# Two latent up-projections on whole float32 operands in place of split halves

## The reference

```
def rmsnorm(x, g):
    x32 = x.astype(jnp.float32)
    y = x32 * lax.rsqrt(jnp.mean(x32 * x32, axis=-1, keepdims=True) + EPS)
    return y.astype(x.dtype) * g
...
        h = rmsnorm(x, pre_norm_mix[l])
        proj = h @ w_in[l]
        g_a, g_b, qa, ka, va, cq, ckv, kr = jnp.split(proj, SPLIT_IDX, axis=-1)
...
        out_a = swa_sink_alibi_attention(qa, ka, va, positions, sinks[l])
        qb = (rmsnorm(cq, q_a_norm[l]) @ w_q_b[l]).reshape(B, S, N_HEADS_B, Q_HEAD_B)
        kvb = (rmsnorm(ckv, kv_a_norm[l]) @ w_kv_b[l]).reshape(B, S, N_HEADS_B, KV_HEAD_B)
        q_nope, q_rope = qb[..., :QK_NOPE], rope(qb[..., QK_NOPE:], positions)
        k_nope, v_b = kvb[..., :QK_NOPE], kvb[..., QK_NOPE:]
        k_rope = rope(kr[:, :, None, :], positions)[:, :, 0, :]
        out_b = mla_attention(q_nope, q_rope, k_nope, k_rope, v_b)
```

## Time and profile before

| what | value |
|---|---|
| median of three runs | 1555.5 us (1555.41 to 1556.49) |
| the profiled execution's own time | 1553.86 us |
| its span | 1552.1 us |
| mean granted TensorE clock | 0.946 |
| busy: PE, DVE, POOL, ACT | 1351.1, 998.1, 628.8, 546.2 us |
| DMA | 397.56 MB, mean 256 GB/s |

### The profile page before, as it was taken

One profiled execution on the slowest core, in us unless ns is written; L12 is line 12 of the kernel. 1 busy time (PEld: TensorE's weight loads), 2 busy tenths in 40 slices (PEclk: granted clock), 3 DMA queues, 4 the chain that ended last, 5 costly groups with the idle time before them and its releaser, 6 DMA issues. The chain is left out here.

```text
span 1552.1 us, 26715 instructions
## 1 busy us (share of the span) xinstructions
PE 1351.1 (87%) x10416; PEld 1296.6 (84%) x10416; DVE 998.1 (64%) x2056; ACT 546.2 (35%) x984; POOL 628.8 (41%) x361
## 2 busy tenths in 40 slices
PE   7989998899898878696888787888898898799996
PEld 6989998898897878696878787888886678689996
DVE  4698946755478585858585859555647565584563
ACT  6444454444432121211112121211564464344341
POOL 1387742221365545454545454542147312122220
PEclk9999999899999989898989898999999999899998
DMA  7445452442359999999999999999342224145450
GB/s 289 148 163 189 172 200 95 163 163 102 114 232 420 422 421 422 422 422 421 422 421 421 420 421 422 422 421 421 139 138 82 82 104 141 50 156 202 164 190 27
DMA packets 58073, 397.56 MB, mean 256 GB/s; under 512 B 6272, under 2 KB 9856, under 8 KB 10368
## 3 DMA queue, kind: packets, MB, share of 16 engines
q0 software_dynamic: 36864, 268.45, 41.6%
q1 hardware_dynamic: 21120, 127.89, 23.2%
HBM read 395.27 MB, written 1.05 MB: 255 GB/s over the span
## 5 line engine op out<-in xcount | busy, mean ns | idle before, releaser
L449 POOL TENSOR_TENSOR w_lo<-raw,w_hi 128x2048 fp32r<-128x2048 f32 x62 | 287.2, 4634 | 570.8 <-ACT w_hi L903 524.2
L761 PE MATMUL bank<-h_norm,rows_late 128*128 128x128 f32 x2816 | 332.8, 281 | 27.1 <-ACT h_norm L1052 27.1
L761 PEld LDWEIGHTS bank<-h_norm,rows_late 128*128 128x128 f32 x2816 | 328.6, 198 | 30.5 <-ACT h_norm L1052 30.5
L1591 DVE SCALAR_TENSOR_TENSOR rows_late<-rows_late,squares 128x1024 f32<-128x1024 f32 x176 | 212.8, 1223 | 131.0 <-DMA rows_late<-peer_uv_dram,stage 129.3
L588 PE MATMUL bank<-x_hi_a,w_hi 128*128 128x256 f32 (+1 forms) x904 | 266.5, 295 | 20.0 <-DVE x_lo_a L1214 11.0
L589 PE MATMUL bank<-x_lo_a,w_hi 128*128 128x256 f32 (+1 forms) x904 | 258.9, 286 | 0.0
L590 PE MATMUL bank<-x_hi_a,w_lo 128*128 128x256 f32 (+1 forms) x904 | 258.9, 286 | 0.0
L761 PE MATMUL bank<-h_norm,rows_early 128*128 128x128 f32 x1280 | 179.5, 309 | 91.0 <-ACT h_norm L1052 90.9
L761 PEld LDWEIGHTS bank<-h_norm,rows_early 128*128 128x128 f32 x1280 | 173.2, 222 | 97.6 <-ACT h_norm L1052 97.6
L530 POOL DMA_INDIRECT rows_late<-peer_uv_dram,stage x165 | 195.1, 1183 | 132.7 <-PE bank L761 95.1
L903 ACT ACTIVATE w_hi<-raw 128x2048 fp32r<-128x2048 f32 (+1 forms) x119 | 224.3, 1887 | 52.7 <-PE bank L590 45.7
(11 more groups left out here) (278 smaller groups left out, 1902.4 us busy)
## 6 DMA issues: line engine op xcount, KB each, us to landing
raw<-w_in_dram SPq DMA_DIRECT2D x40, 1024.0 KB, 4.8
raw<-w_up_dram SPq DMA_DIRECT2D x16, 1024.0 KB, 4.8
raw<-w_down_dram SPq DMA_DIRECT2D x16, 1024.0 KB, 4.8
raw<-w_kv_dram SPq DMA_DIRECT2D x8, 1024.0 KB, 4.7
raw<-w_peer_q_dram SPq DMA_DIRECT2D x8, 1024.0 KB, 4.7
raw<-sc_w_out_dram SPq DMA_DIRECT2D x4, 1024.0 KB, 4.7
raw<-cf_w_pw_dram SPq DMA_DIRECT2D x4, 1024.0 KB, 4.7
raw<-w_mix_out_dram SPq DMA_DIRECT2D x4, 1024.0 KB, 4.8
```

What stands on the lines that cost most here:

```text
L449: api.tensor_tensor(ring(w_lo, i), ring(raw, i), ring(w_hi, i).bitcast(F32), ALU.subtract).then_inc(w_lo_ready[LO_BY[i][0]], 1)
L761: mm = nc.tensor.matmul(ct(Y_ACC[c][t // 4], t % 4, P), expert_rows(k)[:, D + t * P:D + (t + 1) * P], ct(diag, k % DIAGS, P), start=False, ...
L1591: w_.scalar_tensor_tensor(out=row, in0=row, scalar=1.0, in1=h_tok[:, c * D:(c + 1) * D], op0=ALU.mult, op1=ALU.mult, accum_out=pre[:, side ...
```

## The change

Loads 69 and 70 form the set WHOLE. They are still loaded into `raw` at their place in the order, but have no high and no low half. `kn`, `vb` and `qb` are computed by one float32 matmul per k-tile, from `raw` and from the normalised `c_kv` and `c_q`, in place of three float32r matmuls. TensorE now waits for the DMA and for the norm. ACT's two roundings of these loads and its roundings of the latents are gone, and so are DVE's two subtractions of the loads and its subtractions of the latents (`norm` in place of `norm_split`). The condition under which `raw` is filled again changes for the two loads that follow them in their slots, 72 and 73: the DMA waits for the last output tile that reads load 69 (`vb` 3) or load 70 (`qb` 7), in place of the low half. The counts of the semaphores follow (HI_COUNT, LO_BY).

```
--- before.py
+++ after.py
@@ -151,9 +151,14 @@
             + [("w_in_2", b) for b in (2, 3, 4, 5, 6, 7, 11)])
 BY_DVE = range(LOAD_OF["pq", 12], BEFORE_GATHERS + 3)
 
-LO_BY = []
+WHOLE = {i for i, (w, _) in enumerate(LOADS) if w in ("w_kv_b_2", "w_q_b_2")}
+LO_BY, HI_COUNT = [], []
 _seen = {"dve": 0, "pool": 0}
 for _i in range(len(LOADS)):
+    HI_COUNT.append(_i + 1 - sum(w <= _i for w in WHOLE))
+    if _i in WHOLE:
+        LO_BY.append(None)
+        continue
     _e = "pool" if _i % 3 == 2 and _i not in BY_DVE or LOADS[_i] in DVE_BUSY else "dve"
     _seen[_e] += 1
     LO_BY.append((_e, _seen[_e]))
@@ -176,8 +181,7 @@
 
 SPLITS = {"h1": (8, 0, 0, None), "mem": (8, 1, 0, None), "sc": (8, 0, 0, ("gcf", 7)), "pw": (8, 1, 0, ("k", 7)),
           "merge": (8, 0, 0, ("sc", 7)), "xa": (8, 1, 0, ("pw", 7)), "o": (8, 0, 0, ("mix", 7)),
-          "peer": (8, 1, 0, ("q", 7)), "h2": (8, 0, 0, ("xo", 7)), "kv": (1, 1, 0, ("pq", 15)),
-          "q": (2, 1, 1, ("pq", 15)), "oa": (4, 1, 0, ("qb", 7)), "ob": (4, 1, 4, ("qb", 7)),
+          "peer": (8, 1, 0, ("q", 7)), "h2": (8, 0, 0, ("xo", 7)), "oa": (4, 1, 0, ("qb", 7)), "ob": (4, 1, 4, ("qb", 7)),
           "wo": (8, 0, 0, ("gb", 7)), "mlp": (8, 1, 0, ("ob", 7)), "hid0": (FH, 2, 0, None),
           "hid1": (FH, 2, 0, ("down", 7))}
 SPLIT_ENDS = {}
@@ -443,7 +447,7 @@
 
         def w_lo_split(eng, api, i):
 
-            eng.wait_ge(w_hi_ready, i + 1)
+            eng.wait_ge(w_hi_ready, HI_COUNT[i])
             if i >= RING:
                 eng.wait_ge(acc_ready, LAST_TILE[i - RING] + 1)
             api.tensor_tensor(ring(w_lo, i), ring(raw, i), ring(w_hi, i).bitcast(F32),
@@ -461,8 +465,11 @@
                 name, b = LOADS[i]
                 if i >= RING:
 
-                    engine, n = LO_BY[i - RING]
-                    sp.wait_ge(w_lo_ready[engine], n)
+                    if i - RING in WHOLE:
+                        sp.wait_ge(acc_ready, LAST_TILE[i - RING] + 1)
+                    else:
+                        engine, n = LO_BY[i - RING]
+                        sp.wait_ge(w_lo_ready[engine], n)
                 sp.dma_start(ring(raw, i), T[name][b]).then_inc(raw_landed[i % RING], 16)
 
             sp.dma_start(vec[:], T["vecs"]).then_inc(vec_landed, 16)
@@ -504,7 +511,7 @@
 
             def subtract_to(last):
                 while n_lo[0] <= min(last, len(LOADS) - 1):
-                    if LO_BY[n_lo[0]][0] == "pool":
+                    if n_lo[0] not in WHOLE and LO_BY[n_lo[0]][0] == "pool":
                         w_lo_split(pool, g, n_lo[0])
                     n_lo[0] += 1
 
@@ -575,6 +582,12 @@
                 engine, n = LO_BY[i]
                 pe.wait_ge(w_lo_ready[engine], n)
                 return ring(w_hi, i), ring(w_lo, i)
+
+            def whole_slot(name, b):
+
+                i = LOAD_AT[name, b]
+                pe.wait_ge(raw_landed[i % RING], 16 * (i // RING + 1))
+                return ring(raw, i)
 
             def halves(x, k, cols=slice(0, SEQ)):
 
@@ -807,26 +820,28 @@
             linear("qa", range(2), "w_in_2", 8, "h2", DT, 256)
             stat_sq("q_a", mean_q)
             linear("qa", range(2, 4), "w_in_2", 9, "h2", DT, 256)
-            w = slot("w_kv_b_2", 0)
+            w = whole_slot("w_kv_b_2", 0)
+            pe.wait_ge(normed, NORMED["kv_a"])
             for h in range(HB):
                 out = open_tile("kn", h)
-                three(out[0:NOPE, 0:SEQ], [half[:, h * KVHB:h * KVHB + NOPE] for half in w], halves("kv", 0),
-                      True, True).then_inc(acc_ready, 1)
+                nc.tensor.matmul(out[0:NOPE, 0:SEQ], w[:, h * KVHB:h * KVHB + NOPE], c_kv[:],
+                                 start=True, stop=True).then_inc(acc_ready, 1)
             for c in range(NC):
                 for part in range(2):
                     out = open_tile("vb", 2 * c + part)
-                    three(out[:, :], halves("kv", 0, slice(c * P, (c + 1) * P)),
-                          [half[:, part * 512:(part + 1) * 512] for half in w], True, True).then_inc(acc_ready, 1)
+                    nc.tensor.matmul(out[:, :], c_kv[:, c * P:(c + 1) * P], w[:, part * 512:(part + 1) * 512],
+                                     start=True, stop=True).then_inc(acc_ready, 1)
             rot = k_of("rot")[NOPE:QHB, 0:QHB]
             wait_drained(pe, "kr", 0)
             out = open_tile("krot", 0)
             nc.tensor.matmul(out[0:QHB, 0:SEQ], rot, k_r[NOPE:QHB, :], start=True, stop=True).then_inc(acc_ready, 1)
-            w = slot("w_q_b_2", 0)
+            w = whole_slot("w_q_b_2", 0)
+            pe.wait_ge(normed, NORMED["q_a"])
             for h in range(HB):
                 out = open_tile("qb", h)
                 for k in range(2):
                     at = k * HB * QHB + h * QHB
-                    mm = three(out[0:QHB, 0:SEQ], [half[:, at:at + QHB] for half in w], halves("q", k), k == 0, k == 1)
+                    mm = nc.tensor.matmul(out[0:QHB, 0:SEQ], w[:, at:at + QHB], ct(c_q, k), start=(k == 0), stop=(k == 1))
                 mm.then_inc(acc_ready, 1)
 
             def beside_attention(i):
@@ -897,11 +912,13 @@
             def round_to(last):
                 while n_hi[0] <= min(last, len(LOADS) - 1):
                     i = n_hi[0]
+                    n_hi[0] += 1
+                    if i in WHOLE:
+                        continue
                     act.wait_ge(raw_landed[i % RING], 16 * (i // RING + 1))
                     if i >= RING:
                         act.wait_ge(acc_ready, LAST_TILE[i - RING] + 1)
                     s.activation(ring(w_hi, i), ring(raw, i), ACT.Copy).then_inc(w_hi_ready, 1)
-                    n_hi[0] += 1
 
             def normed_tile(norm_name):
                 first = NORMED[norm_name] - dict(NORMS)[norm_name]
@@ -1116,11 +1133,9 @@
                 drain("cq", i, ct(c_q, i))
             root("kv_a")
             square("q_a", drained_tile("cq"), c_q)
-            split_all("kv", normed_tile("kv_a"), c_kv)
             for i in range(2):
                 drain("qa", i, ct(q_a, i))
             root("q_a")
-            split_all("q", normed_tile("q_a"), c_q)
             for i in range(2, 4):
                 drain("qa", i, ct(q_a, i))
             for h in range(HB):
@@ -1242,7 +1257,7 @@
 
             def subtract_to(last):
                 while n_lo[0] <= min(last, len(LOADS) - 1):
-                    if LO_BY[n_lo[0]][0] == "dve":
+                    if n_lo[0] not in WHOLE and LO_BY[n_lo[0]][0] == "dve":
                         w_lo_split(dve, w_, n_lo[0])
                     n_lo[0] += 1
 
@@ -1683,9 +1698,9 @@
             ahead("ka", 0)
             ahead("ckv", 0)
             ahead("cq", 0)
-            norm_split("kv_a", c_kv, "kv_a_norm_2", c_kv, "kv")
+            norm("kv_a", c_kv, "kv_a_norm_2", c_kv)
             ahead("qa", 0)
-            norm_split("q_a", c_q, "q_a_norm_2", c_q, "q")
+            norm("q_a", c_q, "q_a_norm_2", c_q)
             ahead("qa", 2)
             ahead("kn", 0)
 
```

## The result

The changed kernel takes 1564.39 us (median of six runs, 1561.31 to 1570.94), the kernel before on the same chips 1556.28 us (six runs, 1555.41 to 1560.46). The ratio is 1.0054, with a 95% interval from 1.0037 to 1.0072. So it is slower by about 8 us, where 7.0 were forecast. A second set of six runs of the same file gave 1566.28 us and 1.0053 [1.0037, 1.0068].

What follows compares the result with a forecast made beforehand. TensorE's own work was taken to set the end of the stage. 5.3 us of stall, including 2.1 for float32 matmuls, plus 1.7 for the clock gave +7.0: 1562.5 us on the median, 8-in-10 range 1557.8 to 1566.

Steps and rivals of the forecast that it cites:

- The float32 pairs: In `kn`, `vb` and `qb`, two float32 matmuls replace three float32r ones: 0.43 against 0.36 us for narrow tiles, +2.1 us showing.
- the pause of 1.16 us: TensorE's wait ahead of `kn` 4 for ACT, which rounds load 71 first; it hides 0.3 us of the first four tiles.
- The four passes: Alternative price for the float32 matmuls in `kn`, `vb` and `qb`: four passes instead of three, 3.7 us in all; not adopted.
- The chain of steps 1 to 6: Last `vb` matmul, DMA of load 72, ACT's rounding, drain of `qb` 0, then `qb` 4: +5.3 us, matmuls' 2.1 included.
- the landing: Load 72's DMA, issued at 1149.4 behind `vb` 3, lands 4.8 us later at the median, at most 5.0.
- the clock: TensorE's 3.1 us pause in `qb` lowers its granted clock behind it: +1.7 us, bounds 0 and 3.4.
- the attention: Behind the changed stage, attention, output layers and MLP only shift along, since nothing downstream is tied to an absolute time.
- The rival of the clock that keeps its level: The wait in `qb` comes but the clock stays up in `qb` 4 to 7: +5.3 us, 1560.8 us; chance 0.2.
- the rival "faster": Attention gives time back and load 72's transfer costs less than its 4.8 us: 1553 to 1555 us; chance 0.04.
- The second late transfer: Loads 73, 74 and 75 issue together around `qb` 7; load 73 lands late, losing 1 to 4 us more; chance 0.14.
- The delay given back: In the attention, POOL's subtraction shifts against head a 1's scores, TensorE's 3.42 us gap shrinks: +1.9 us, 1557.4; chance 0.12.

Runs made afterwards that it cites:

- own buffers: Changed kernel with the two whole weights loaded into idle buffers of their own, so `raw` is refilled early again: 1559.93 us, ratio 1.0019 to the kernel before.
- The late refill without float32: Kernel before, keeping all its halves, with only loads 72 and 73 made to wait for the last tile of loads 69 and 70: 1562.75 us, ratio 1.0042.
- The drain put first: Changed kernel, load 72 still late, but ACT rounds it behind the drains of `qb`: 1563.1 us, ratio 1.003 to the kernel before.
- `w_kv_b_2` alone: Changed kernel with only `w_kv_b_2` multiplied whole, `w_q_b_2` and its latent keeping their halves: 1561.8 us, ratio 1.0029 to the kernel before.
- seven fillers: Changed kernel with seven useless float32 matmuls of zeros between `qb` 3 and `qb` 4: 1564.93 us, ratio 1.0051 to the kernel before.
- the one run with `neg_max` at 0.23 us: Kernel before with the low half of load 73 made by DVE in place of POOL: 1554.16 us, ratio 0.9984.
- eleven fillers: Changed kernel with eleven useless float32 matmuls of zeros between `qb` 3 and `qb` 4: 1562.62 us, ratio 1.0037 to the kernel before.
- own buffers and the drains of `kn` first: Changed kernel with separate buffers for both whole weights and ACT rounding load 71 behind the `kn` drains: 1559.63 us, ratio 1.0022 to the kernel before.

## Why the prediction was right, and where it was off

Sign and mechanism held, and the median came out near the forecast: +7.0 us forecast, about +8 measured. That it came so near is in part luck. For the profiled execution 1560.9 us were forecast and 1570.94 measured, and in both traces of the changed kernel the stage and the attention together are 13.4 and 14.1 us longer, since three terms were set too low. Step by step:

- **The float32 pairs.** Forecast 0.43 us each and +2.1 us that show; measured 0.44 us (7.07/16) in `qb`, and +2.42 us in the stage of own buffers (0.44 for `kn`, 0.79 for `vb`, 1.27 for `qb`, less 0.08). `kn` 4 to 7 took 0.47 us each, start-up included, so tiles of 64 and 96 rows cost nearly what L619's of 128 rows do. As forecast, the pause of 1.16 us shrank, to 0.66, and took the price of `kn` 0 to 3. (The "2.5 before the pause is taken off" is 2.4 by the prediction's own three terms.)
- **The four passes.** The Trainium skill, page "FP8 and Floating Point Precision", section "TensorE Precision Notes", says four passes for true float32. Here one float32 matmul cost 0.44 us against 0.36 us for three float32r ones, 1.22 times as much and not 4/3, so going by the rows (+2.1) was closer than the estimate by passes (3.7).
- **The chain of steps 1 to 6.** Every link is in the trace, the first scores at 1165.1 on that clock excepted (forecast 1160 to 1162): issue at 1153.13, 3.6 us earlier on the clock of the trace before (1149.5, forecast 1149.4), ACT idle for the DMA, rounding, drain, `qb` 4. The late refill without float32 shows that it needs nothing else of the change. The drain put first shows that it acts through ACT's order, and own buffers that it goes when the refill is early again.
- **Mis-sized: the landing.** The step "The DMA is issued at 1149.4 and lands 4.8 us later at the median, at most 5.0" had 6.8 us in one trace and 7.6 in the other. That makes the gap 4.86 and 5.67 us, not 3.1. Bytes were not shared with another load, since none was on the way. It took long in all five traces with both operands whole and the load late (6.8, 7.6, 6.7, 6.7 and 5.9 us), and 4.8 us with `w_kv_b_2` alone and with the late refill alone. The DMA view from 1153.0 to 1160.2, in 40 slices of 0.18 us (busy tenths, then GB/s), shows that most bytes had moved after 4.4 us and the last ones came a packet at a time:

```profile
DMA  4000039422859599979999632010110101010000
GB/s 91 0 0 0 0 46 319 91 46 46 273 228 501 228 410 364 501 319 410 410 410 501 228 137 91 0 46 0 46 46 0 46 0 46 0 46 0 0 0 0
```

- **Mis-sized: the clock.** Forecast +1.7 us out of 0 to 3.4; the low stretch held for 6.8 us, and `qb` 4 to 7 took 6.55 us instead of 3.54, +3.0 us. I had taken the stretch of 3.4 us behind the gap at 1212 instead of the one of 6.9 us at 1168. The Trainium skill, page "TensorE: Matmul & The Clock Gate", section "Why this matters for your kernels", warns of such gaps. Here the traces agree: 2.5 to 3.0 us behind gaps of 3.38 to 5.67 us, and nothing behind the rest of 1.71 us that seven fillers left. They show falls behind much shorter gaps too, in the attention (last section), which that advice doesn't cover, and there the traces decide.
- **Missed: the attention.** "Downstream nothing is tied to an absolute time" is where the forecast failed. In the changed kernel the attention is 2.9 us longer, with the second stretch of low clock behind a gap of 1.53 us. The gap at that place before was 1.30 us, with the clock at 1.00. The two rows, after and before:

```profile
1198.25 0.66 PE L682 MATMUL bank<-const,probs 128*128 128x128 f32 x4 [1.53 <-DVE probs L1474]
...
1184.18 0.66 PE L669 MATMUL bank<-const,probs 128*128 128x128 f32 x4 [1.30 <-DVE probs L1459]
```

- **The rival of the clock that keeps its level** (1560.8) is refuted in both traces, and the rival "faster" by the sign.
- **The second late transfer** is refuted. Loads 73, 74 and 75 went out together, but load 73 landed after 4.9 us, the next after 7.0 and the last after 9.0. ACT's rounding of load 73 starts at 1174.47 right behind the exponentials, without a wait for the DMA.
- **The delay given back** is refuted. `neg_max` of head a 1 takes 1.98 us again, ahead of a gap of 3.42 us again. Its premise stays untested: in the one run with `neg_max` at 0.23 us the gap shrank by 0.74 us only, to 2.68 and not to 1.7, as DVE's own subtraction came in its place. The clock fell behind 2.68 us all the same.

The sum in the stage, +10.45 us: 2.42 for the matmuls, 5.02 for the stall (1153.62 to 1162.18 less 3.54) and 3.01 for the clock. By the ratios, the kernel with own buffers costs 3.0 us (in its trace not by the matmuls alone) and the late refill alone 6.5; together that is 9.5, where 8.1 to 8.4 were measured, within what the intervals allow.

**What stays open.** Why the landing took 5.9 to 7.6 us with both operands whole: in these traces a packet of 16 KB of the queue that fetches instructions lies beside the issue, but one also lies there with the late refill alone, where 4.8 us sufficed. Why the second stretch of low clock comes: it is there after the change, with own buffers and with seven fillers, and not with eleven fillers, with the late refill alone, with one operand whole, or with own buffers and the drains of `kn` first. The engines' rows in the 30 us ahead of it agree within 0.3 us with those before. And why both profiled executions of the changed kernel were the longest of their sets: whether the unprofiled ones had shorter landings or shorter low stretches no trace here can show.

## What to carry to other kernels

A copy or a split of an operand also frees the buffer that it was loaded into. Read the operand directly and the refill moves from the split to the last matmul, so ask which load comes next into that slot, who waits for it, and what stands behind that wait in an in-order list. Here ACT rounded that load ahead of its drains, and one late load, 4.8 to 7.6 us from issue to landing, became a stop of TensorE, with half its clock for some microseconds behind.

A whole operand cost nothing measurable where its successor was not needed next, and 4.5 us where it was. Float32 in place of three float32r products is no gain on TensorE (1.22 times the time), and what it saved on the other engines bought nothing that a run here shows, as TensorE sets the end.
